# Even mixer: both attentions as one chain of 64 units in one written-out order, latent set-up in the index chain's bank

## The reference, cut to what matters

```python
h = x @ w_in                       # 1024 -> q_a, c_kv, q_idx, k_idx, w_idx, q_b, k_b, v_b, f_in
q_lat = einsum('bshd,hrd->bshr', q_a, w_uk) * 64 ** -0.5      # 8 heads, rank 128
for each block i of 128 queries:
    score = einsum('bth,bths->bts', w_idx, relu(q_idx . k_idx))   # index score, 8 heads
    sel = top_k(where(causal, score, -inf), 128)                 # 128 keys for each query
    # "latent" attention: only over the selected keys
    la = q_lat . c_kv[sel] + rel_bias[t5_bucket(distance)];  oa = softmax(la) . c_kv[sel]
    # "forget" attention: over all earlier keys
    lb = q_b . k_b + cum_f(query) - cum_f(key);  ob = softmax(lb) . v_b
o_a = einsum('bshr,hrd->bshd', oa, w_uv)
return concatenate([o_a, ob]) @ w_o
```

## Time and profile before

| | us |
|---|---|
| median of 3 runs | 2035.05 |
| lowest, highest | 2032.69, 2035.78 |
| the profiled execution | 2035.01 |
| its span | 2032.9 |
| the even mixer in it: first step of the walk to the output projection's first matmul | 761.5 to 1042.6 |

### The profile page before, as it was taken

The page is one execution under the profiler, slowest core; times in us unless marked ns, Lnnn a source line. Parts: engine busy times, 40 slices in busy tenths (PEclk is TensorE's granted clock), DMA queues, the critical chain, the costliest instruction groups (busy, mean ns, idle before and its releaser), DMA issues.

```text
span 2032.9 us, 24275 instructions
## 1 busy us (share of the span) xinstructions
PE 1951.4 (96%) x10214; PEld 1588.6 (78%) x10214; DVE 971.7 (48%) x1551; ACT 732.2 (36%) x1229; POOL 243.9 (12%) x166
## 2 busy tenths in 40 slices
PE   5999979999999999989999999999999999999998
PEld 5778967888888887557678888888788588888886
DVE  3665454332332245763456655533663266555434
ACT  4654343322221243435553443421232124434311
POOL 0433410011110023101000111100000001111000
PEclk9999979999999999769999999999999699999999
DMA  4211003223223232101012223233223022232321
GB/s 148 101 52 64 23 20 132 79 88 104 100 94 100 96 107 102 40 23 42 1 63 83 98 88 104 100 107 104 99 83 125 21 83 98 89 104 100 118 88 68
DMA packets 28225, 169.80 MB, mean 84 GB/s; under 512 B 3355, under 2 KB 5059, under 8 KB 10324
## 3 DMA queue, kind: packets, MB, share of 16 engines
q1 hardware_dynamic: 28118, 168.27, 24.2%
HBM read 166.12 MB, written 2.11 MB: 83 GB/s over the span
## 4 chain that ended last, share of the span: by engine, by line
PE 87%; DVE 10%; ACT 1%; issue 1%; DMA 1%; SPq 0%; DVEq 0%; ACTq 0%
PE ps L585 25%; PE ps L586 24%; PE ps L587 24%; PE ps L1070 1%; DVE sco L2248 1%; DVE m L2246 1%; PE ps L1038 1%; PE ps L1195 1%; PE ps L1194 1%; DVE wL L1806 1%; DVE x L2338 1%; PE ps L1121 1%; DVE hL L1812 1%; PE ps L1082 1%; PE ps L1060 1%
## 5 line engine op out<-in xcount | busy, mean ns | idle before, releaser
L585 PE MATMUL ps<-hH,wH 128*128 128x512 f32 (+1 forms) x1568 | 613.6, 391 | 7.9 <-DVE hL L1812 4.9
L587 PE MATMUL ps<-hH,wL 128*128 128x512 f32 (+1 forms) x1568 | 595.2, 380 | 0.0
L586 PE MATMUL ps<-hL,wH 128*128 128x512 f32 (+1 forms) x1568 | 595.1, 380 | 0.0
L1806 DVE TENSOR_TENSOR wL<-raw,wH 128x1024 fp32r<-128x1024 f32 (+1 forms) x252 | 307.3, 1260 | 393.1 <-ACT wH L1295 393.1
L1295 ACT ACTIVATE wH<-raw 128x1024 fp32r<-128x1024 f32 (+2 forms) x298 | 290.3, 1023 | 304.7 <-PE ps L587 304.6
L585 PEld LDWEIGHTS ps<-hH,wH 128*128 128x128 f32 x1568 | 299.3, 191 | 74.6 <-issue 11.4
L587 PEld LDWEIGHTS ps<-hH,wL 128*128 128x128 f32 x1568 | 298.9, 191 | 55.4
L586 PEld LDWEIGHTS ps<-hL,wH 128*128 128x128 f32 x1568 | 299.7, 191 | 52.3 <-issue 2.3
L585 PE MATMUL ps<-wH,aH 128*128 128x512 f32 x528 | 209.0, 396 | 0.0
L586 PE MATMUL ps<-wL,aH 128*128 128x512 f32 x528 | 208.8, 395 | 0.0
L587 PE MATMUL ps<-wH,aL 128*128 128x512 f32 x528 | 208.8, 395 | 0.0
(11 more groups left out here) (372 smaller groups left out, 1864.4 us busy)
## 6 DMA issues: line engine op xcount, KB each, us to landing
raw<-in_wbig SPq DMA_DIRECT2D x139, 1024.0 KB, 4.9
rows<-in_rows SPq DMA_DIRECT2D x12, 512.0 KB, 5.9
x<-in_x SPq DMA_DIRECT2D x8, 512.0 KB, 5.8
raw<-in_wbig SPq DMA_DIRECT2D x8, 512.0 KB, 3.6
out<-x SPq DMA_DIRECT2D x4, 512.0 KB, 2.6
near<-u_scratch SPq DMA_DIRECT2D x1, 1024.0 KB, 7.5
raw<-in_wbig SPq DMA_DIRECT2D x1, 1000.0 KB, 7.6
raw<-in_wbig SPq DMA_DIRECT2D x1, 600.0 KB, 10.7
```

The costliest lines, as they stand in the source:

```text
L585: e.matmul(o, hi, m_hi, start=first, stop=False)
L586: e.matmul(o, hi, m_lo, start=False, stop=False)
L587: return e.matmul(o, lo, m_hi, start=False, stop=end)
L1806: e.tensor_tensor(wL[r][:, cs], raw[r][:, cs], wH[r][:, cs].bitcast(F32), ALU.subtract).then_inc(*low_dve.one(c, h))
```

## The change

1. **The order.** `even_order` returns one string of 444 letters in place of the planner's result: 156 F, 96 I and 192 A. `weave` remains for another stage.
2. **One chain of attention units.** `units` runs over 64 units: 0 to 31 forget, 32 to 63 latent, both in the walk. All are scored three ahead, have four slots, and put their products in bank 6 alone. The latent attention's own run behind the walk is gone.
3. **Latent set-up in the index chain.** After the searches, the index chain issues for each head `ql` and `near`, and for head 0 the four `va`, all in bank 7.
4. **Dense work moved.** The second half of the values (`vb`) is now chunk 56 (`C_V2`), inside the walk behind the index keys; it was chunk 52, ahead of the walk. The small columns are chunk 52.
5. **The turns.** The four turns of `otb` are the last four F steps of the walk, in banks 0 and 1. The four turns of `ota` come inside the output projection, one after each token group of chunk 63, in banks 4 to 7. Chunk 63 reads only the turned `otb`.
6. GpSimd fills the far part of `mb` within the walk, and SP fetches the rows of the layer norm after unit 63 instead of after the last turn.

The number of multiplications, copies and transposes stays as it was.

```diff
-def even_order():
-    index = [(300, 3000, 0), (0, 9000, 0), (0, 6000, 0)]
-    for i in range(1, 4):
-        index += [(250 * (i + 1), 900, 50)] * 8 + [(0, 700, 0)] * 16
-    index += [(0, 0, 0)]
-    units = unit_steps(3, lambda h: 8 * (7 + 2 * (h // 2)) + 9)
-    return weave([690.0] * 144, {"I": index, "A": units})
+def even_order():
+    return ("FFFFFIFFFFFFFFFFFFFFFFFFFFFIFFFFFFFFFFFFFFFFIFFFFFFFIFIFFIFIFIFIFIFIFFFIFFIIFFIIIIFFFFIIFFFFIFIIFAFIFFFIIIFFIFFIAFAFFAIA"
...
# TensorE, index chain, behind the third search
+                for h in range(8):
...
+                    e.matmul(ps[7][:, :], wuk[r, h // 2, :], qaT[h // 2][r, :], start=True, stop=True).then_inc(*lat.pe.one("ql", h))
+                    bank[7] = [lat.act.at("ql", h)]
+                    yield
+                    clear(7)
...
+                    e.matmul(ps[7][:, 0:256], anti[:, :], near[:, h, :], start=True, stop=True).then_inc(*lat.pe.one("near", h))
+                    bank[7] = [lat.dve.at("bias", h, 3)]
+                    yield
...
# TensorE, the chain of units
+                for n in range(-3, 64):
+                    if n + 3 < 64:
+                        u = n + 3
+                        b = 2 + u % 2
+                        clear(b)
+                        score = latent_score if u >= 32 else forget_score
...
-                        b, v = product(h, n)
-                        clear(b)
-                        w.wait_ge(*m.act.at("turn", n))
...
+                        v = va if n >= 32 else vb
+                        clear(6)
+                        w.wait_ge(*unit.act.at("turn", n))
...
-            walk(EVEN_ORDER, F=dense_even(), I=index(), A=forget())
...
-            run(units(lat, slots_a, 4, score_a, product_a))
-            for j, o, m in ((1, otb, fgt), (0, ota, lat)):
-                for i in range(4):
-                    turn("mix", i, o[:, i, :], [m.act.at("o", 28 + i)], (j,))
...
+            walk(EVEN_ORDER, F=dense_even(), I=index(), A=units())
...
-            turn3 = ln_stage(0, [63, 64], [65, 66], hH, hL, of_mixed)
+            turn3 = ln_stage(0, [63, 64], [65, 66], hH, hL, of_mixed, True, {i: lambda i=i: turn_a(i) for i in range(4)})
```

More of the change, by code:

```diff
@@ L240, in run @@
         pass
[L243 to L253, removed]
 def first_order():
@@ L1004, in vb_emptied, with turn_b, turn_a @@
                 return lambda i: [even.act.at("vb", i, half)]
[L1006 to L1009, removed]
+            run(tok([C_EVEN], True, hH, hL, of_turn("res"), [0, 1, 0, 1], vb_emptied(0), {(1, 0): lambda: turn_res(3)}))
+            run(feat(C_SMALL, [0], "res", lambda t: [even.dve.at("wx")]))
+            def turn_b(i):
+                turn("mix", i, otb[:, i, :], [unit.act.at("o", 28 + i)], (1,), i % 2)
+            def turn_a(i):
+                turn("mix", i, ota[:, i, :], [unit.act.at("o", 60 + i)], (0,), 4 + i)
             def dense_even():
@@ L1063, in units @@
+                        t.then_inc(*unit.pe.one("turn", n + 1))
+                        bank[b] = [unit.act.at("turn", n + 1)]
                         yield
                     if n >= 0:
[L1065 to L1068 removed]
+                        h, i = n % 32 // 4, n % 4
+                        if n < 32:
+                            for j in range(4):
+                                w.wait_ge(*even.act.at("vb", j, h // 4))
+                        else:
+                            w.wait_ge(*lat.act.at("va", 3))
@@ L1073, in units @@
+                        t.then_inc(*unit.pe.one("o", n))
+                        bank[6] = [unit.act.at("o", n)]
                         yield
[L1075 to L1081, removed]
-                    return e.matmul(ps[b][:, 0:128 * (i + 1)], QB[:, h, 128 * i:128 * i + 128], KB[:, h, 0:128 * (i + 1)], start=True, stop=True)
-                def product(h, n):
-                    for j in range(4):
-                        w.wait_ge(*even.act.at("vb", j, h // 4))
-                    return 6 + n % 2, vb
-                yield from units(fgt, slots_b, 3, score, product)
-                yield "done"
@@ L1668, in units @@
+                        w.wait_ge(*unit.dve.at("rec", n))
+                        if n >= 32:
+                            w.wait_ge(*unit.pe.at("score", 31))
+                        o = ota if n >= 32 else otb
+                        e.activation(o[:, i, 64 * h:64 * h + 64], ps[6][:, 0:64], ACT.Copy, scale=sx2[:, n % 4, 2:3]).then_inc(*unit.act.one("o", n))
                         yield
-            def forget():
-                yield from units(fgt, slots_b, 3, lambda n: None, lambda u: even_start(), otb)
@@ L1687, in first_a, with ln_stage @@
-            def first_a(n):
-                if n == 0:
-                    latent(0)
-                if n % 4 == 1 and n < 28:
-                    latent(n // 4 + 1)
-            run(units(lat, slots_a, 4, first_a, lambda u: [fgt.pe.at("o", 30 + u)], ota))
-            for j in (1, 0):
-                for i in range(4):
-                    turn("mix", i, (j,))
-            def ln_stage(n, a, b, turns=True):
+            walk(EVEN_ORDER, F=dense_even(), I=index(), A=units())
+            def ln_stage(n, a, b, turns=True, early={}):
```

353 lines of the change are left out of this document (180 added, 173 removed).

## The result

The changed kernel takes 1983.26 us (median of 4 runs, 1981.26 to 1985.87), the kernel before 2034.58 us (4 runs, 2032.69 to 2035.78): ratio 0.9749, 95% interval 0.9732 to 0.9766, a gain of 51.3 us. Two more sets of runs gave 1983.05 (ratio 0.9749, 0.9736 to 0.9763) and 1984.27 us (0.9754, 0.9741 to 0.9767); the kernel before against itself gave 1.000 (0.9991 to 1.0009). The forecast was 1993 us, its range began at 1987: the direction and the main mechanism (the waits go, and the slow clock with them) were right, the gain was 9 us larger and lies outside the range.

The account below looks back on a forecast made before the run. It took VectorE as the bound in the even mixer's searches, with TensorE waiting and its clock falling. 48.5 us gained, less 2 + 2 + 1.5 and 1, gave 42 us: 1993 us, range 1987 to 2010 (main case 1988 to 1999).

Parts of the forecast that it names:

- What bounds the kernel: Even mixer, first index score to third search's end: VectorE bounds at 98 us against TensorE's 83; waits bring slow clock.
- The sum of TensorE's work: Even mixer: TensorE's work is 232.6 of 281.1 us, so 48.5 us are lost, the most the change can gain.
- TensorE's 132 us against VectorE's 115: New order's work before sel 3 is reached: the bound moves from VectorE to TensorE.
- less 2 + 2 + 1.5 and 1 for what I can't see: New waits in the even mixer, taken off the 48.5 us to leave a 42 us gain.
- The 2 us for the third search: New waits in the second and third search rounds, cover only just enough in the third: 2 us, ends 0 and 8.
- Three units ahead, 2 us: Latent heads: scoring three units ahead instead of four leaves 512-wide units short of cover; 2 us, ends 1 and 8.
- ScalarE at the turns, 1.5: Walk's last dozen steps: four turns give ScalarE 7 us beside 6 on TensorE; 1.5 us of wait.
- The clock: Even mixer: if the waits go, all 29 us lost to slow clock come back.
- One stretch of 20 to 25 us costs 10 to 12 us: Rival, third round: one wait leaves a slow stretch, its wait costing 3 us more; 2006 us (1999 to 2012), chance 0.20.
- Bank 7: Latent set-up: cost nought; rival: 20 issues wait 0.69 us each, 14 us, units' products likewise, 2007 to 2020, chance 0.07.
- The half-clock tail: Rival: last 60 to 70 us of the walk, few dense steps, run at half clock; 2065 us, chance 0.04.
- The order does nothing: Rival: an engine falls behind in the searches as before, only tail and turns gain 5 to 10 us; 2027, chance 0.05.

Follow-up runs that it names:

- old_order: Changed kernel with the planner's old order written out, latent units without dense steps between, turns last; new structure kept: 2049.16 us, ratio 1.0075.
- the added maxima: Four kernels: the changed kernel with 4, 8, 12 or 24 more VectorE maxima in the third search: 1985.72, 1990.61, 1992.93 and 2000.23 us.
- latent_last_banks: latent_last with `ql` in bank 0 and the bias table in bank 1, as before the change: 1995.92 us, ratio 0.9812.
- latent_last: Changed kernel, new order to the end of the third search, then remaining dense and forget steps, then latent heads alone, then turns: 2008.41 us, ratio 0.9874.
- before_again: The kernel before, unchanged, run again for a second profile: 2033.69 us.

## Why the prediction was wrong, point by point

- **What bounds the kernel: right for the waits, too wide for the stretch.** In before, VectorE is busy in 94% of the wait of 5.5 us, so it sets the pace there. Yet from the first index score to the third mask it is busy in only 70% (87.9 of 125 us), less than the 74% of after. Behind the wait the bound is TensorE itself at half clock. Both in before, as length, busy PE, PEld, DVE, ACT, POOL:

```profile
866.80:872.40 5.60, 0.07 (x2) 0.05 (x1) 5.26 (x16) 1.33 (x4) 0.00 (x0) 0.82 0.00 0
...
880.00:890.00 10.00, 10.00 (x19) 4.33 (x18) 2.79 (x9) 2.38 (x6) 0.00 (x0) 0.50 0.00 0
```

  That the clock's loss hangs on the waits fits: old_order brings both back with the old order alone, and the added maxima bring them one at a time.
- **The sum of TensorE's work, 232.6 us of 281.1: right.** With 48.5 us off, the mixer should be 299.8 - 48.5 = 251.3 us with its turns. Measured are 249.9 + 1.8 = 251.6, of which 0.4 is the one new wait. That it is so near is partly luck: taken from each matmul's start to the next one's in the trace of after, the 144 dense steps make 108 us against the 97.7 put down, the index scores 20 against 25.9, the units 84 against 88.3, set-ups and `va` 15 against 16.9. Part of this is that a dense step behind other work takes longer than one in a row of dense steps (its first matmul 0.28 us on average, the third 0.24, in a row 0.23), a cost that I had in the price of the index scores.
- **TensorE's 132 us against VectorE's 115 up to the third mask: the first right, the second too high.** The row of 783.6 to 917.2 shows 133.6 us and 99.4 us busy. VectorE is therefore at 74% there, not above 80%; TensorE is at 100%. The 115 us also hold the gaps between the search's small instructions, so they can't be set against the 99.4 directly; with the units' price below, I put them at 103.
- **The step that failed: "less 2 + 2 + 1.5 and 1 for what I can't see".** These 6.5 us of new waits measured 0.4. Of the 9.7 us between 1993 and 1983.3, this is 6.1; the other 3.6 are the 3.1 by which the medians moved more than the mixer, and 0.5 by which before's median came out lower. (1) The 2 us for the third search rest on a unit's 1.0 us on VectorE, which I had called a bound from above and then used as the price. The timeline of VectorE in the third search of after: maxima (L2224), strikings-out (L2226), a 512-wide and a 128-wide unit between (L2265 and the small ones behind it):

```profile
906.38 0.68 DVE L2226 MATCH_REPLACE8 sco<-m,sco 128x512 f32<-128x512 f32 x1
906.98 0.68 DVE L2265 CUSTOM_DVE_ANT_0 rows<-ps,CM 128x512 f32<-128x512 f32 x1
907.58 0.08 DVE L2265 DVE_READ_ACCUMULATOR2_ANT sx<- 128x1 f32 x1
907.70 0.15 DVE L2267 TENSOR_SCALAR sx<-sx 128x1 f32<-128x1 f32 x1
907.77 0.15 DVE L2272 RECIPROCAL sx<-sx 128x1 f32<-128x1 f32 x1
907.84 0.67 DVE L2224 MAX8 m<-sco 128x8 f32<-128x512 f32 x1
...
908.63 0.68 DVE L2226 MATCH_REPLACE8 sco<-m,sco 128x512 f32<-128x512 f32 x1
909.22 0.28 DVE L2265 CUSTOM_DVE_ANT_0 rows<-ps,CM 128x128 f32<-128x128 f32 x1
...
909.69 0.68 DVE L2224 MAX8 m<-sco 128x8 f32<-128x512 f32 x1
...
910.48 0.68 DVE L2226 MATCH_REPLACE8 sco<-m,sco 128x512 f32<-128x512 f32 x1
911.19 0.69 DVE L2224 MAX8 m<-sco 128x8 f32<-128x512 f32 x1
```

  Without a unit the next maximum starts 0.71 us after the striking-out (911.19 - 910.48). With the 512-wide unit it is 1.46 (907.84 - 906.38), with the 128-wide one 1.06 (909.69 - 908.63): the units cost the search 0.75 and 0.35 us, since the unit's short instructions start 0.07 to 0.12 us apart and its first one starts where the search had its gap. Taking 0.6 for the mean of the widths, 31 units cost 19 us and not 31; so VectorE has 12 us less to do than I counted. Nine of these units stand in the third search, 3.6 us less there by this estimate, which is most of the way from the 2 us I charged to the 2.5 to spare. (2) Three units ahead, 2 us: no wait. latent_last_banks shows that it isn't the work between that saves it: where the latent units stand without dense steps, 940 to 990 us, TensorE is idle for 0.17 us. (3) ScalarE at the turns, 1.5: measured 0.4. (4) What I couldn't see, 1: nothing.
- **The low end of the range failed with it.** 1987 stood for "all 48.5 us", that is, no new wait at all, on one profiled execution whose time was the median. No new wait was the outcome that came, and nothing was left below it for the scatter outside the mixer, which gave 1 to 3 us more.
- **The clock: right in the forecast, wrong in the rival's price.** All of the 29 us came back. "One stretch of 20 to 25 us costs 10 to 12 us" is not what a lone wait cost in the new order: that is 3 us. In before, a wait of 2.4 us and one of 5.5 us were followed by 20 and 27 us of half clock, although no wait above 0.4 us came within them (the row of 880 to 890 above lies in the second). In before, TensorE had 512- and 384-wide index scores among its work behind these waits, in the new order none. Whether that is the reason was not tested; the price was right for the old order.
- **Bank 7: right here, and the rival was real.** With units between, no set-up waits. Without them each `ql` costs 0.69 us, as latent_last shows, plus `mb` and slow clock: 12.5 us in all. The Trainium skill (Perfetto Trace Analysis, Optimizing Tensor Performance, Matmuls) advises rotating independent groups through different banks; latent_last against latent_last_banks agrees, after itself shows that other work in between does as well.
- **The half-clock tail: refuted.** From 930 to 985 us units with few dense steps ran at 1.00. The Trainium skill (TensorE: Matmul & The Clock Gate, Part 4: PE-mode transpose) says that transposes don't count as busy for the clock gate as matmuls do. No run here tests that: this tail and the one in the earlier trace rows have other matmuls among the ten transposes of each head, so the full clock speaks against the rival that was built on the page, and not against the page.
- **Chunk 63 starts without a gap: right** (990.51 + 1.10 against 991.43; a record's end reaches into the next). **The order does nothing: refuted,** it is the part that pays.

## What to carry to other kernels

When a change only reorders, add up the bottleneck engine's own work from the timeline: the difference to the stretch's length is the whole gain that can be had (here right to 0.3 us in sum, with terms that were off by up to 10), and an order searched for it can reach nearly all of it. Charge a new wait only where the cover worked out from measured starts, not from busy times alone, is really too small, and don't let the range end at the case "no new wait". Test a structural part with the old order, and an order with the old banks: the new structure alone was 15 us slower than before.

## What the runs showed of the hardware

- **In the third search of the new order, a lone wait of 3 to 15 us on TensorE costs about 3 us of half clock behind it** (2.6 to 3.3, one profile each), whatever its length. This is no general price. In before, waits of 2.4 and 5.5 us were followed by 20 and 27 us of half clock. In latent_last a 1.6 us wait followed by several of 0.69 us (926 to 946 us) kept the clock at 0.50 to 0.57 for 20 us.
- **Short waits mostly cost no clock, but not always.** `va`'s three waits of 0.69 us alone (latent_last_banks, 920 to 940) and six behind `ql` (latent_last, 950 to 1013) left it at 1.00. The 1.5 us wait ahead of the walk stands in twelve profiles. In eleven the clock stayed full behind it, in before_again 3.4 us of half clock followed:

```profile
760.00:770.00 10.00, 9.96 (x38) 7.87 (x39) 8.33 (x5) 5.21 (x7) 4.88 (x2) 0.83 0.62 210
```

  And behind waits of 0.17, 0.27 and 0.40 us the clock fell for 10 us in latent_last_banks and stayed full in latent_last. What tells these cases apart I did not settle.
- **Half clock doesn't need idle time.** In a later stage, untouched by the change, TensorE is busy without a gap and yet at 0.50; 17 to 19 us are lost there in every kernel. Its cause was not examined. The stage in the changed kernel:

```profile
1530.00:1560.00 30.00, 30.00 (x99) 14.01 (x98) 5.94 (x9) 3.45 (x6) 0.00 (x0) 0.50 0.00 0
```

- **Scatter in steps.** Executions of one kernel differ by 1.7 us or a multiple of it in clock loss at much the same places: 0, 1.7 or 3.4 us in the first 30 us and around 1420, 17.1 or 18.8 in the stage above, 0 or 1.7 behind the small columns in before. A difference of 3 us between two kernels' medians may be only that.
